# Moving the tail of a long depthwise convolution into a state space chunk loop, and taking the two halves of an output projection in the other order

## The chip, the cores and the metric

One core of one Trainium2 chip runs the whole program. The metric is the device time of one execution in microseconds (us), the median of several runs.

## What is computed

Two transformer blocks, for 256 tokens of width 1024. The change touches the mixer of the second block alone. Cut to that:

```python
def ssd_mixer(z, xbc, dt_raw, conv_w, conv_b, dt_bias, a_log, d_skip, norm_w):
    xbc = silu(causal_depthwise_conv(xbc, conv_w, conv_b))        # 4 taps
    xs, bm, cm = split(xbc, [1024, 1536])
    dt = softplus(dt_raw + dt_bias)
    y = ssd_chunked(xs, dt, -exp(a_log), bm, cm)                  # chunks of 128 tokens, 16 heads in 4 groups
    y = (y + d_skip * xs) * silu(z)
    yg = y.reshape(b, l, 4, 256)
    yg = yg * rsqrt(mean(yg * yg, -1) + EPS)                      # one norm per group of 256 columns
    return yg.reshape(b, l, 1024) * norm_w

def conformer_conv(u, conv_w, conv_b, ln_g, ln_b):
    a, g = split(u, 2)
    h = causal_depthwise_conv(a * sigmoid(g), conv_w, conv_b)     # 31 taps
    return silu(layer_norm(h) * ln_g + ln_b)                      # over all 1024 columns

def second_block(x, ...):
    proj = rmsnorm(concat([meta, x])) @ w_in                      # z, xbc, dt, conformer input
    h = h + concat([y_ssd, y_conf], -1) @ w_out                   # 2048 x 1024
    h = h + peer_ffn(rmsnorm(h), ...)
```

The rest (a first block with attention and a feed forward, then the expert layer with its 16384 experts) is as it was.

## The kernel before, in words

Activations lie transposed: 128 partitions of columns, 256 (or 272, with 16 meta tokens) tokens along a row, so 1024 columns are 8 tiles. All weights stream through in 423 **units** of 128x1024 numbers in one fixed order. SyncE loads a unit into one of four buffers (`load_weights`, L268), ScalarE rounds it to its high part (`hi_to`, L907), VectorE subtracts to get the low part (`lo_to`, L1360), and TensorE makes three products of high and low parts for each 128x128 block (`three`, L302 to L304), 24 matmuls of 256 tokens to a unit. Three slots `W` hold converted units: ScalarE may convert unit u when TensorE has ended unit u-3, and SyncE may load unit u when VectorE has ended unit u-4. Each engine has one program, written out by hand; nothing reorders it. An engine that waits holds up all that stands behind it.

The mixer's stages, in the order of the program (times of the next sections are from the profile's start):

- Units U_ZA, U_GLU, U_XB (40 units) make z, the conformer input `GP` and xbc. Beside them VectorE starts the long convolution: `long_convs` (L1609), one instruction of 128x256 per tap and tile, 156 in all. 18 of the 31 taps of tiles 4 and 5, and all of tiles 0 to 3, are VectorE's. TensorE does the other 88 taps (`PE_TAPS`: 13 of tiles 4 and 5, all 31 of tiles 6 and 7) as fp32 products with diagonal matrices (`conv_taps`, L615), which ScalarE makes (`diagonals`, L1145) from a ring of `NDIAG` = 64.
- The step sizes dt (L628, L1648 to L1655), their decays (L634 to L636), and then for the three pieces of tokens (16, 128, 128) the transposes of xs and B (L647, L656), scaled by VectorE (L1669, L1676), each followed by taps on TensorE (`tap(8)`) and on VectorE (`some_taps`).
- Chunk states (L673, copied at L1210, combined at L1684, L1687).
- The last taps; the layer norm of the conformer half: column sums for the mean (L682), subtraction (L1694), squares (L914), their sums (`column_sums`, L310), root (L920), inverse (L1366), scaling (L1698), silu and high part (L1222, L1224), low part (L1702).
- The **chunk loop**, n = 0 to 9: `core_a(n)` (L717 to L725) makes decay sums and C times B for one of 8 (group, chunk) pairs, ScalarE takes exponentials (L1235, L1237), VectorE multiplies (L1711, L1716), `core_b(n-1)` (L742, L744) makes the outputs, VectorE adds the skip and the gate (L1727, L1732). Between `core_a` and `core_b` stands one unit of the conformer half of the output projection (`conformer_units`). Every second turn a group is complete: squares, `group_sum` (L753), root, inverse, scaling (L1739), high and low part (L1251, L1742).
- Then the 8 units of the state space half of the output projection, which add into the same four accumulators ps0 to ps3, and the residual sum (L1749). The query projection (U_WQ) follows.

The lines that set the order around the change:

```python
            for n in range(10):
                if n < 8:
                    core_a(n)
                if n in (0, 1, 2, 4, 5, 6, 8, 9):
                    next(conformer)
                if 1 <= n < 9:
                    core_b(n - 1)
                if n >= 3 and n % 2:
                    group_sum((n - 3) // 2)
            for m in range(8):
                weights(U_OS + m)
```

## Time and profile before

| | |
|---|---|
| median of 3 runs | 1465.0 us (1464.36 to 1465.64) |
| the profiled execution | 1464.91 us, span 1462.8 us |
| TensorE busy | 1402.1 us, 96% of the span |
| VectorE busy | 1072.0 us, 73% |
| ScalarE busy | 736.5 us, 50% |
| the stretch that the change edits | 489 to 630 us of the span |

### The profile page before, as it was taken

Reading aid. Unit: us, or ns where it says so; the run is one execution under the profiler, and the core shown is the slowest. Engines: PE = TensorE matmul, PEld = TensorE weight load, DVE = VectorE, ACT = ScalarE, POOL = GpSimd, SP = SyncE. Lnnn points to the kernel's source line nnn. Section 1 sums busy time; section 2 is a strip of 40 time slices with the busy share of each in tenths; the row PEclk is TensorE's granted clock in tenths of the full one; section 3 lists DMA queues with packets and bytes.
Section 4 is the critical chain, followed back from the end, with each engine's and each line's share of the span. In section 5 each row is a group of like instructions: output and inputs, shape, how many; then the busy total and the mean of one; then the engine's idle time right before and its main releaser. Section 6 shows DMA issues by size and latency. Waiting matters only on the chain.

```text
span 1462.8 us, 25179 instructions
## 1 busy us (share of the span) xinstructions
PE 1402.1 (96%) x10456; PEld 1281.1 (88%) x10456; DVE 1072.0 (73%) x1742; ACT 736.5 (50%) x1051; POOL 3.1 (0%) x8
## 2 busy tenths in 40 slices
PE   6999899997999989899999999999999999999997
PEld 6978799997999867899999999999987777888886
DVE  7654766447799866677899986888878888655554
ACT  6755555445567535466544445443444344444443
POOL 0000000000000000000000000000000000000000
PEclk9999899998999899999999999999999999999999
DMA  7423355663555002355555555555455555656653
GB/s 259 157 73 106 116 183 177 210 191 103 183 162 168 18 0 73 101 174 160 175 185 188 173 188 182 166 167 165 159 172 163 171 163 169 180 191 201 188 186 105
DMA packets 63617, 228.59 MB, mean 156 GB/s; under 512 B 7312, under 2 KB 8208, under 8 KB 63376
## 3 DMA queue, kind: packets, MB, share of 16 engines
q1 hardware_dynamic: 63072, 226.25, 48.7%
q8 instruction: 82, 1.34, 0.4%
q10 hardware_dynamic: 432, 0.74, 0.1%
q14 instruction: 31, 0.25, 0.1%
HBM read 225.91 MB, written 1.05 MB: 155 GB/s over the span
## 4 chain that ended last, share of the span: by engine, by line
PE 89%; DVE 6%; ACT 4%; issue 1%; DMA 0%; DVEq 0%; ACTq 0%
PE ps L302 17%; PE ps L304 17%; PE ps L303 17%; PE ps L870 8%; PE ps L872 8%; PE ps L871 8%; PE ps L615 2%; PE ps L836 2%; DVE W L1360 1%; DVE RSI L1366 1%; PE ps L352 1%; ACT W L907 1%; PE ps L354 1%; PE ps L498 1%; PE ps L360 1%
## 5 line engine op out<-in xcount | busy, mean ns | idle before, releaser
L1360 DVE TENSOR_TENSOR W<-raw,W 128x1024 fp32r<-128x1024 f32 x423 | 515.6, 1222 | 275.1 <-ACT W L907 273.7
L907 ACT ACTIVATE W<-raw 128x1024 fp32r<-128x1024 f32 x423 | 446.3, 1057 | 393.7 <-PE ps L872 208.4
L302 PE MATMUL ps<-XH,W 128*128 128x256 f32 (+1 forms) x1552 | 442.4, 285 | 3.1 <-DVE hid L1780 2.0
L303 PE MATMUL ps<-XL,W 128*128 128x256 f32 (+1 forms) x1552 | 439.8, 283 | 0.0
L304 PE MATMUL ps<-XH,W 128*128 128x256 f32 (+1 forms) x1552 | 437.7, 282 | 0.0
L302 PEld LDWEIGHTS ps<-XH,W 128*128 128x128 f32 x1552 | 291.9, 188 | 5.0 <-DVE hid L1780 2.2
L304 PEld LDWEIGHTS ps<-XH,W 128*128 128x128 f32 x1552 | 294.0, 189 | 0.0
L303 PEld LDWEIGHTS ps<-XL,W 128*128 128x128 f32 x1552 | 292.6, 188 | 0.0
L870 PE MATMUL ps<-W,HH 128*128 128x512 f32 x512 | 205.7, 402 | 0.8 <-ACT hid L1325 0.8
L872 PE MATMUL ps<-W,HL 128*128 128x512 f32 x512 | 203.1, 397 | 0.0
L871 PE MATMUL ps<-W,HH 128*128 128x512 f32 x512 | 203.0, 397 | 0.0
L872 PEld LDWEIGHTS ps<-W,HL 128*128 128x128 f32 x512 | 96.5, 188 | 23.4
L870 PEld LDWEIGHTS ps<-W,HH 128*128 128x128 f32 x512 | 96.5, 188 | 23.0 <-issue 1.0
L871 PEld LDWEIGHTS ps<-W,HH 128*128 128x128 f32 x512 | 96.6, 189 | 22.0
L1325 ACT ACTIVATE hid<-ps 128x512 f32<-128x512 f32 x64 | 38.3, 598 | 115.1 <-PE ps L304 115.1
L302 PE MATMUL ps<-F1H,W 128*128 128x256 f32 x256 | 70.7, 276 | 0.0
L303 PE MATMUL ps<-F1L,W 128*128 128x256 f32 x256 | 70.7, 276 | 0.0
L304 PE MATMUL ps<-F1H,W 128*128 128x256 f32 x256 | 70.7, 276 | 0.0
L1609 DVE SCALAR_TENSOR_TENSOR plain<-plain,vec 128x256 f32<-128x256 f32 x156 | 64.9, 478 | 0.5 <-DVE small L1651 0.5
L1893 DVE TENSOR_TENSOR onehot<-RSI 128x1024 f16<-128x1024 f16 x64 | 44.2, 691 | 16.8 <-PE ps L836 15.7
L304 PEld LDWEIGHTS ps<-F1H,W 128*128 128x128 f32 x256 | 48.1, 188 | 0.0
L302 PEld LDWEIGHTS ps<-F1H,W 128*128 128x128 f32 x256 | 48.1, 188 | 0.0
(327 smaller groups left out, 1997.7 us busy)
## 6 DMA issues: line engine op xcount, KB each, us to landing
raw<-in_w_dn SPq DMA_DIRECT2D x128, 512.0 KB, 3.5
raw<-in_w_up SPq DMA_DIRECT2D x128, 512.0 KB, 3.5
raw<-in_w_ff SPq DMA_DIRECT2D x64, 512.0 KB, 4.3
raw<-in_w_in SPq DMA_DIRECT2D x57, 512.0 KB, 3.7
raw<-in_w_out SPq DMA_DIRECT2D x24, 512.0 KB, 3.4
raw<-in_w_q SPq DMA_DIRECT2D x16, 512.0 KB, 3.6
raw<-in_w_kv SPq DMA_DIRECT2D x4, 512.0 KB, 3.4
plain1a<-in_memT SPq DMA_DIRECT2D x1, 1024.0 KB, 10.8
```

Of the source, the lines that this page charges most:

```text
L302: e.matmul(out, wh, xh, start=first, stop=False, skip_group_check=shared)
L303: e.matmul(out, wh, xl, start=False, stop=False, skip_group_check=shared)
L304: return e.matmul(out, wl, xh, start=False, stop=last, skip_group_check=shared)
L615: e.matmul(ps[7 if j < 6 else 0][:, half(j)], DIAG[:, p % NDIAG, :], GP[:, j, 16 + k:272 + k], start=k == 0, stop=p + 1 == len(PE_TAPS) or ...
L870: e.matmul(ps[b][:, :], HH[:, c % 8, tok], wh, start=c == 0, stop=False)
L871: e.matmul(ps[b][:, :], HH[:, c % 8, tok], wl, start=False, stop=False)
L872: return e.matmul(ps[b][:, :], HL[:, c % 8, tok], wh, start=False, stop=c == 127)
L907: e.activation(W[:, u % NSLOT, 0, :], raw[:, u % NRAW, :], ACT.Copy).then_inc(s["hi"], 1)
L1325: e.activation(hid_[:, 256 * c - 256:256 * c + 256], ps[(c // 2) % 4][:, :], ACT.Gelu).then_inc(s["gl"], 1)
L1360: e.tensor_tensor(W[:, u % NSLOT, 1, :], raw[:, u % NRAW, :], W[:, u % NSLOT, 0, :], ALU.subtract).then_inc(s["lo"], 1)
L1609: e.scalar_tensor_tensor(CV[:, j, :], GP[:, j, 16 + k:272 + k], V("ccw", 31 * j + k), CV[:, j, :], ALU.mult, ALU.add).then_inc(cv[j], 1)
L1893: e.tensor_tensor(OA, pairs(IOTA, 128), at(0, 128), ALU.is_equal).then_inc(s["oa"], 1)
```

## The change

Nothing is computed otherwise; the same instructions stand in another order, in other buffers, but for two.

- The units' order: the state space half `U_OS` now precedes the conformer half `U_OC`.
- TensorE's taps: 18 (was 14) before the decays, none (was 12) after them, 5 (was 8) behind each of six transposes, and 6 in each turn of the chunk loop where a conformer unit stood, until the 88 are done in turn 6. Their banks are ps0 and ps1; `NDIAG` is 32 and ScalarE makes 1 diagonal per unit (was 2), then 10, 8, 6 and 6 per turn.
- VectorE's taps: 3 and 2 where 8 and 5 stood, none (was 12) before the states; then 2 + 2 in each turn of the loop, and the last 6 in turn 7.
- `LT` and `CM`, the loop's exponentials, get a place of their own (they lay in `CV`, the convolution's result), where `XH` and `XL` lie at other times.
- The loop has 9 turns and no projection unit. Group 0's and 1's roots are taken together in turn 5 (two table loads on ScalarE for both), group 2's in turn 8, group 3's behind the loop.
- Behind the loop come the state space units (`mixed_units`), one tile of activations after the other over all 8 output tiles. Between them stand the layer norm's mean (behind the first), group 3's sum (behind the second) and the squares' sums (behind the third), and on VectorE and ScalarE the rest of the layer norm and of groups 2 and 3 beside the units' conversions. The conformer units come last.

```diff
-U_ZA, U_GLU, U_XB, U_OC, U_OS, U_WQ, U_SK, U_DN, U_UP, NU = 93, 101, 117, 133, 141, 149, 165, 167, 295, 423
+U_ZA, U_GLU, U_XB, U_OS, U_OC, U_WQ, U_SK, U_DN, U_UP, NU = 93, 101, 117, 133, 141, 149, 165, 167, 295, 423
-NDIAG = 64
+NDIAG = 32
...
-            tap(14)
+            tap(18)
             e.wait_ge(s["dt_v"], 3)
...
-            tap(12)
...
-                    tap(8)
+                    tap(5)
...
+            def mixed_units():
+                for c in range(8):
+                    weights(U_OS + c)
+                    if c == 0:
+                        for j, n in ((4, 13), (5, 13), (6, 31), (7, 31)):
+                            e.wait_ge(cv[j], n)
+                        e.wait_ge(s["rs"], N_G + 2)
+                    if c % 2 == 0:
+                        e.wait_ge(s["yc_l"], c // 2 + 1)
                     for k in range(8):
+                        t = three(ps[k // 2][:, half(k)], slot(U_OS + c, slice(k * 128, k * 128 + 128)),
+                                  (YCH[:, c, :], YCL[:, c, :]), c == 0 and k % 2 == 0, False, True)
...
-            for n in range(10):
+            for n in range(9):
                 if n < 8:
                     core_a(n)
-                if n in (0, 1, 2, 4, 5, 6, 8, 9):
-                    next(conformer)
-                if 1 <= n < 9:
+                tap(6)
+                if n >= 1:
                     core_b(n - 1)
                 if n >= 3 and n % 2:
                     group_sum((n - 3) // 2)
+            tap(len(PE_TAPS))
+            mixed = mixed_units()
+            next(mixed)
+            layer_mean()
+            next(mixed)
+            group_sum(3)
+            next(mixed)
+            e.wait_ge(s["ltm"], 8)
+            column_sums(6, 256, HT, SQ_LN)
+            for _ in mixed:
+                pass
...
# VectorE, in the loop
+                some_taps(2)
+                if n >= 1:
...
+                some_taps(2)
+                if n == 5:
+                    group_norm(0)
+                if n == 6:
+                    group_low(0)
+                    group_norm(1)
+                if n == 7:
+                    group_low(1)
+                    for _ in convs:
+                        pass
```

**Order, place 1: VectorE in one turn of the chunk loop.** Before, turn 1 (L1711, L1716: products with the exponentials; L1360: low part of a conformer unit; L1727, L1732: skip and gate):

```order
L1711 TENSOR_TENSOR plain2<-plain2,ps6 128x512 [waits c_c,lt]
L1716 TENSOR_TENSOR plain2<-plain2 128x512 [waits cm]
L1360 TENSOR_TENSOR W<-raw,W 128x1024 [waits hi]
L1727 SCALAR_TENSOR_TENSOR plain2<-plain2,vec,ps7 128x128 [waits c_b]
L1727 SCALAR_TENSOR_TENSOR plain2<-plain2,vec,ps7 128x128
L1732 TENSOR_TENSOR plain2<-plain2 128x2x128 [waits cy]
```

Now, turn 1 (L1733, L1738, L1747 and L1752 are the same four; L1637 is a tap of the long convolution, of tiles 4 and 5):

```order
L1733 TENSOR_TENSOR LT<-LT,ps6 128x512 [waits c_c,lt]
L1738 TENSOR_TENSOR CM<-CM,plain2 128x512 [waits cm]
L1637 SCALAR_TENSOR_TENSOR plain2<-plain2,vec 128x256 [waits cv4]
L1637 SCALAR_TENSOR_TENSOR plain2<-plain2,vec 128x256 [waits cv5]
L1747 SCALAR_TENSOR_TENSOR plain2<-plain2,vec,ps7 128x128 [waits c_b]
L1747 SCALAR_TENSOR_TENSOR plain2<-plain2,vec,ps7 128x128
L1752 TENSOR_TENSOR plain2<-plain2 128x2x128 [waits cy]
L1637 SCALAR_TENSOR_TENSOR plain2<-plain2,vec 128x256 [waits cv4]
L1637 SCALAR_TENSOR_TENSOR plain2<-plain2,vec 128x256 [waits cv5]
```

The unit's conversion has gone, and two taps stand ahead of the wait for `c_b`, two behind the gate.

**Order, place 2: VectorE from the taps into the layer norm.** Before (L1694: the layer norm's subtraction; L1366, L1698: its inverse and scaling; L1702: low parts; L1711: first product of the chunk loop):

```order
L1609 SCALAR_TENSOR_TENSOR plain2<-plain2,vec 128x256 [waits cv5]
L1609 SCALAR_TENSOR_TENSOR plain2<-plain2,vec 128x256 [waits cv4]
L1609 SCALAR_TENSOR_TENSOR plain2<-plain2,vec 128x256 [waits cv5]
L1694 SCALAR_TENSOR_TENSOR plain2<-ps2,plain2 128x256 [waits ln_mm]
L1694 SCALAR_TENSOR_TENSOR plain2<-ps2,plain2 128x256 x7
L1366 RECIPROCAL RSI<-RSI 128x256 [waits rs]
L1698 SCALAR_TENSOR_TENSOR plain2<-plain2,vec,RSI 128x256 [waits ri]
L1698 SCALAR_TENSOR_TENSOR plain2<-plain2,vec,RSI 128x256 x7
L1702 TENSOR_TENSOR YCL<-plain2,YCH 128x512 [waits yc_h] x4
L1711 TENSOR_TENSOR plain2<-plain2,ps6 128x512 [waits c_c,lt]
```

Now, from the last turns on (L1747, L1752: last skip and gate; L1394, L1720: inverse and scaling of group 2; L1771: the layer norm's subtraction; L1725: group 2's low part):

```order
L1637 SCALAR_TENSOR_TENSOR plain2<-plain2,vec 128x256 [waits cv5]
L1637 SCALAR_TENSOR_TENSOR plain2<-plain2,vec 128x256 [waits cv4]
L1637 SCALAR_TENSOR_TENSOR plain2<-plain2,vec 128x256 [waits cv5]
L1747 SCALAR_TENSOR_TENSOR plain2<-plain2,vec,ps7 128x128 [waits c_b]
L1747 SCALAR_TENSOR_TENSOR plain2<-plain2,vec,ps7 128x128
L1752 TENSOR_TENSOR plain2<-plain2 128x2x128 [waits cy]
L1394 RECIPROCAL RSI<-RSI 128x256 [waits rs]
L1720 SCALAR_TENSOR_TENSOR plain2<-plain2,vec,RSI 128x256 [waits ri]
L1720 SCALAR_TENSOR_TENSOR plain2<-plain2,vec,RSI 128x256
L1771 SCALAR_TENSOR_TENSOR plain2<-ps5,plain2 128x256 [waits ln_mm]
L1771 SCALAR_TENSOR_TENSOR plain2<-ps5,plain2 128x256 x7
L1725 TENSOR_TENSOR YCL<-plain2,YCH 128x512 [waits yc_h]
```

The last taps moved behind the products of the last chunk, and between them and the layer norm's subtraction stand now the last skip and gate and the norm of group 2.

**Order, place 3: TensorE where the state space half begins and where a unit changes its accumulator.** Before, a unit of the projection in the loop, its end, `core_a` and the next unit's start (L302 to L304: the three products of a block; L717 to L725: `core_a`):

```order
L302 MATMUL ps0<-YCH,W 128x256
L303 MATMUL ps0<-YCL,W 128x256
L304 MATMUL ps0<-YCH,W 128x256
L717 MATMUL ps4<-plain2,cstb 128x512 [waits lt]
L718 MATMUL ps4<-MASK 128x512
L722 MATMUL ps5<-plain2,cst 128x512 [waits cm]
L725 MATMUL ps6<-plain2 128x128 [waits ltm]
L302 MATMUL ps0<-YCH,W 128x256 [waits lo]
L303 MATMUL ps0<-YCL,W 128x256
L304 MATMUL ps0<-YCH,W 128x256
```

Now, the end of the last `core_b` (L739, L741) and the first state space unit (L309 to L311 are the three products):

```order
L739 MATMUL ps7<-LT,plain2 64x128
L741 MATMUL ps7<-CM,plain2 64x128
L309 MATMUL ps0<-YCH,W 128x256 [waits cv7,cv6,rs,cv5,yc_l,cv4,lo]
L310 MATMUL ps0<-YCL,W 128x256
L311 MATMUL ps0<-YCH,W 128x256
L309 MATMUL ps0<-YCH,W 128x256
L310 MATMUL ps0<-YCL,W 128x256
L311 MATMUL ps0<-YCH,W 128x256
L309 MATMUL ps1<-YCH,W 128x256
L310 MATMUL ps1<-YCL,W 128x256
```

The first unit waits for the copies of the diagonal taps' sums, the third group's root and group 0's low part; the output half changes with every block and the accumulator with every second, where it was one accumulator for two whole units.

## Rows read from the trace of the kernel before

**Rows 1.** Section 1 of the page: busy us (share of the span) and instructions.

```profile
PE 1402.1 (96%) x10456; PEld 1281.1 (88%) x10456; DVE 1072.0 (73%) x1742; ACT 736.5 (50%) x1051; POOL 3.1 (0%) x8
```

**Rows 2.** Timeline of PE, decays to chunk loop (start, us, line, forms, [idle before <-releaser]).

```profile
489.85 7.12 PE L615 MATMUL ps<-plain,diag 128*128 128x256 f32 x24
496.81 0.60 PE L647 MATMUL ps<-cst,plain 128*16 128x128 f32 x4
497.24 3.62 PE L615 MATMUL ps<-plain,diag 128*128 128x256 f32 x16
500.70 0.60 PE L647 MATMUL ps<-cst,plain 128*16 128x128 f32 x4
...
521.14 3.91 PE L673 MATMUL ps<-plain 16*128 16x256 f32 x16
...
536.15 3.69 PE L310 MATMUL ps<-plain,cst 128*128 128x256 f32 x16 [1.60 <-ACT plain L914]
539.68 1.02 PE L717 MATMUL ps<-plain,cstb 128*128 128x512 f32 x2
```

**Rows 3.** Timeline of DVE: last taps behind the states, an inverse, a scaling.

```profile
526.95 2.06 DVE L1609 SCALAR_TENSOR_TENSOR plain<-plain,vec 128x256 f32<-128x256 f32 x5
...
569.03 1.75 DVE L1366 RECIPROCAL RSI<-RSI 128x256 f32<-128x256 f32 x1 [0.31 <-ACT RSI L920]
570.82 0.88 DVE L1739 SCALAR_TENSOR_TENSOR plain<-plain,vec,RSI 128x256 f32<-128x256 f32 x2
```

**Rows 4.** Timeline of PE, one turn of the chunk loop with its unit.

```profile
557.76 1.12 PE L717 MATMUL ps<-plain,cstb 128*128 128x512 f32 x2
...
559.94 0.36 PE L302 MATMUL ps<-YCH,W 128*128 128x256 f32 x1
...
562.86 0.45 PE L742 MATMUL ps<-plain 128*64 128x128 f32 x4
...
563.93 1.13 PE L717 MATMUL ps<-plain,cstb 128*128 128x512 f32 x2
```

**Rows 5.** Timeline of DVE, skip, gate and the next turn's products.

```profile
564.04 0.61 DVE L1727 SCALAR_TENSOR_TENSOR plain<-plain,vec,ps 128x128 f32<-128x128 f32 x2 [1.24 <-PE ps L744]
564.68 0.42 DVE L1732 TENSOR_TENSOR plain<-plain 128x256 f32<-128x256 f32 x1
...
566.46 0.69 DVE L1711 TENSOR_TENSOR plain<-plain,ps 128x512 f32<-128x512 f32 x1 [1.35 <-PE ps L725]
```

**Rows 6.** Timeline of ACT, a run of diagonals.

```profile
497.79 7.11 ACT L1145 ACTIVATE diag<-cst,vec 128x128 f32<-128x128 f32 x24
```

**Rows 7.** Waits of PE, 489 to 631 us (us in total, times, longest).

```profile
PE ps L302 <- DVE YCL L1702: 4.2, 1, 4.2
PE ps L302 <- DVE YCL L1742: 2.6, 1, 2.6
```

**Rows 8.** Windows (stretch; us, busy us by engine, granted clock, DMA share, GB/s).

```profile
535.00:540.00 5.00, 3.85 (x17) 3.34 (x18) 2.33 (x8) 2.64 (x5) 0.00 (x0) 1.00 0.01 3
...
545.00:550.00 5.00, 3.82 (x18) 3.85 (x18) 2.80 (x6) 4.82 (x12) 0.00 (x0) 0.50 0.00 0
...
608.20:613.20 5.00, 4.95 (x29) 4.95 (x30) 2.45 (x2) 1.28 (x2) 0.00 (x0) 0.66 0.38 116
...
127.80:139.40 11.60, 11.60 (x92) 10.38 (x90) 5.83 (x10) 5.63 (x12) 0.00 (x0) 1.00 0.43 136
```

**Rows 9.** Timeline of PE, two units, second to last matmul: mixed order, then one accumulator.

```profile
143.23 0.28 PE L303 MATMUL ps<-MXL,W 128*128 128x256 f32 x1
...
145.83 0.28 PE L304 MATMUL ps<-MXH,W 128*128 128x256 f32 x1
...
553.98 0.28 PE L303 MATMUL ps<-YCL,W 128*128 128x256 f32 x1
...
556.48 0.28 PE L304 MATMUL ps<-YCH,W 128*128 128x256 f32 x1
```

**Rows 10.** Timeline of DVE, the last residual sum.

```profile
629.93 0.69 DVE L1749 TENSOR_TENSOR X<-ps,X 128x512 f32<-128x512 f32 x1 [0.34 <-PE ps L304]
```

More of the change, by code:

```diff
@@ L159, in build @@
         P2b = stack()
-        DIAG = tensor(P2b, "diag", [128, NDIAG, 128])
+        diag_ = tensor(P2b, "diag", [128, 64, 128])
+        DIAG = [diag_[:, (16 if i < 16 else 32) + i, :] for i in range(NDIAG)]
         P2b.close()
@@ L166, in build @@
         DTU = [plain2[:, at:at + 2048].rearrange("p (a b) -> p a b", b=128) for at in (8 * 272, 16 * 272)]
-        LT, CM = (CV[:, 4 * i:4 * i + 4, :].rearrange("p (s a) b -> p s (a b)", s=2) for i in range(2))
         xb0 = 24 * 272 + 8 * 302 + 2048
@@ L1168, in scalar_program @@
                         conv_first(t)
-                for _ in range(2):
-                    next(diags)
+                next(diags)
             for m in range(16):
@@ L1179, in scalar_program, with diagonal @@
                                      scale=V("scw", 4 * i)).then_inc(s["xi"], 1)
-                for _ in range(2):
-                    next(diags)
+                next(diags)
+            def diagonal(n):
+                for _ in range(n):
+                    next(diags, None)
             for i in range(0, 16, 2):
@@ L1210, in scalar_program, with group_root, group_high @@
                 e.activation(PREV[0][:, hf * 512:hf * 512 + 512], ps[st_bank[hf]][:, :], ACT.Copy).then_inc(s["st_a"], 1)
-            conv_out(6, 31)
-            conv_out(7, 31)
-            sqrt_table()
+            def group_root(g):
+                root(N_G + g, g_bank[g], 256, 1.0 / 256, eps5, g % 2, 1 if g == 0 else 2)
+            def group_high(g):
+                for i in range(2):
+                    e.wait_ge(s["gn"], 2 * g + i + 1)
+                    e.activation(YCH[:, 2 * g + i, :], YC[:, 2 * g + i, :], ACT.Copy).then_inc(s["yc_h"], 1)
+            for n in range(9):
+                if n < 8:
+                    if n >= 2:
+                        e.wait_ge(s["c_b"], n - 1)
+                    e.wait_ge(s["c_d"], n + 1)
+                    e.activation(LT[:, n % 2, :], ps[4][:, :], ACT.Exp).then_inc(s["lt"], 1)
+                    e.wait_ge(s["c_a"], n + 1)
+                    e.activation(CM[:, n % 2, :], ps[5][:, :], ACT.Exp).then_inc(s["cm"], 1)
+                    diagonal(6)
+                if n == 2:
+                    hi_to(U_OS + 3)
+                if n == 5:
+                    group_root(0)
+                    group_root(1)
+                if n in (6, 7):
+                    group_high(n - 6)
+                if n == 7:
+                    conv_out(6, 31)
+                    conv_out(7, 31)
+                if n == 8:
+                    group_root(2)
+                if n >= 2 and n % 2 == 0:
+                    g = n // 2 - 1
+                    e.wait_ge(s["cy"], 6 * g + 6)
+                    square(SQ2[:, 2 * g:2 * g + 2, 0:256], YC[:, 2 * g:2 * g + 2, :])
+            group_high(2)
             for c in range(0, 8, 2):
                 e.wait_ge(s["ln_v"], c + 2)
-                square(SQ2[:, c:c + 2, 0:256], CV[:, c:c + 2, :])
-            root(N_LN, 3, 256, 1.0 / 1024, eps5)
+                square(HT[:, c:c + 2, 0:256], CV[:, c:c + 2, :])
+            hi_to(U_OS + 4)
+            group_root(3)
+            hi_to(U_OS + 5)
+            group_high(3)
+            hi_to(U_OS + 6)
+            root(N_LN, 6, 256, 1.0 / 1024, eps5, 0, 2)
             for j in range(8):
@@ L1733, in vector_program @@
                                     ALU.mult).then_inc(s["cy"], 1)
[L1734 to L1743 removed]
+                some_taps(2)
@@ new lines, in vector_program @@
+                if n == 2:
+                    lo_to(U_OS + 3)
+                if n == 5:
+                    group_norm(0)
+                if n == 6:
+                    group_low(0)
+                    group_norm(1)
+                if n == 7:
+                    group_low(1)
+                    for _ in convs:
+                        pass
+            group_norm(2)
+            e.wait_ge(s["ln_mm"], 1)
+            for j in range(8):
+                e.scalar_tensor_tensor(CV[:, j, :], ps[5][:, 0:256], -1.0 / 1024, CV[:, j, :], ALU.mult,
+                                       ALU.add).then_inc(s["ln_v"], 1)
@@ new lines, in vector_program @@
+            group_low(2)
+            lo_to(U_OS + 4)
+            group_norm(3)
+            lo_to(U_OS + 5)
+            group_low(3)
+            lo_to(U_OS + 6)
+            inverse(N_LN, 256)
+            for j in range(8):
+                e.scalar_tensor_tensor(CV[:, j, :], CV[:, j, :], V("lng", j), RI[:, 0, 0:256], ALU.mult,
+                                       ALU.mult).then_inc(s["ln_n"], 1)
+                if j in (3, 7):
+                    lo_to(U_OS + 7 + j // 4)
+            for j in range(0, 8, 2):
+                e.wait_ge(s["yc_h"], 8 + j + 2)
+                e.tensor_tensor(YCL[:, 8 + j:10 + j, :], CV[:, j:j + 2, :], YCH[:, 8 + j:10 + j, :],
+                                ALU.subtract).then_inc(s["yc_l"], 1)
```

174 lines of the change are left out of this document (60 added, 114 removed).

## The prediction

> **What bounds the kernel now.** I read the page first: TensorE is busy 96% of the span and VectorE 73% [rows 1], so a change of order can only win what TensorE loses between its matmuls. Next the windows and waits of the stretch that is edited: in 489 to 631 us TensorE waits 4.2 us once and 2.6 us once for low parts [rows 7], and behind each of these gaps its clock is granted at half for a while: 0.50 in 545 to 550 us, 0.66 in 608.2 to 613.2 us [rows 8]. Last the timelines of PE and DVE, which give every duration below. What the reader is to see in them: from 521.14 to 539.68 us TensorE does the last taps and the layer norm's sums, 18.5 us, for a chunk loop that needs none of it [rows 2]; and the loop then runs at TensorE's own pace, 6.17 us a turn [rows 4]. The layer norm's chain of short steps on three engines has nothing beside it but the start of the loop, and the last group's chain has nothing beside it at all.
>
> **The sum** is a new timetable for TensorE from 489.3 us (decays done) to its last matmul of the output projection, which is at 629.7 us now (0.2 to 0.3 us ahead of the residual sum that waits for it [rows 10]). Outside, nothing changes its length: ScalarE makes 32 diagonals fewer beside the units, where it isn't what is waited for; TensorE's four more taps ahead of the decays (1.7 us) end about when VectorE has the step sizes (the decays' products are through at 489.85 now, where the next taps start [rows 2]; I take 489.3 for both). Table loads on ScalarE fall by three, one comes back beside the query projection; both lie beside longer TensorE work, so I cost them at nothing. The DMA queue keeps its waits (unit u behind the low part of u-4); the new order gives it long stretches to fill four buffers, so nothing there either.
>
> *Prices.* A tap on TensorE: 8 in 500.70 - 497.24 = 3.46 us, 0.433 each. Four transposes: 497.24 - 496.81 = 0.43 us [rows 2]. A tap on VectorE: 2.06 / 5, 0.40 with pipelining. Inverse 1.75, scaling 0.88 [rows 3]. `core_a`: 559.94 - 557.76 = 2.18; a unit's 24 matmuls 2.72 (0.1135 each [rows 9]); `core_b`: 563.93 - 562.86 = 1.07 us [rows 4]. A product with an exponential 0.60, skip 0.6, gate 0.42 [rows 5]. A diagonal 7.11 / 24 = 0.30 [rows 6]. Handing over from TensorE to VectorE: 564.04, where the skip starts, against 563.93, where TensorE goes on behind the products it needs, so 0.1 and what one product of 64 rows takes: 0.25, an estimate.
>
> *A. Decays to chunk states.* Now 489.3 to 521.14 = 31.9 us, with 12 + 48 taps. The change leaves 30: 30 x 0.433 = 13.0 less, 18.9. VectorE's own chain here (two large products, then scalings with 3 or 2 taps between them) I walked through beside it: it holds the third transpose group back by some 0.3 net. 19.2 us: **-12.7**.
>
> *B. States to the first `core_a`.* Now 521.14 to 539.68 = 18.5 us. The new `core_a` waits for VectorE's fourth combination, which ended where its next taps start, 526.95 - 521.14 = 5.8 us behind the states' start [rows 2, 3]; with the hand-over 6.0: **-12.5**. TensorE idles 2.1 of them.
>
> *C. Chunk loop.* Now 539.68 to 608.25 us = 68.6 us, the second 2.6 us wait included, and 0.75 of a state space unit is done in it. New: turn 0 2.18 + 6 x 0.433 = 4.8; turns 1 to 5 each 2.18 + 2.60 + 1.07 = 5.85, 29.3; two group sums 1.7; turn 6 with 4 taps 5.0; turn 7 with a group sum 4.1; that is 44.9 us. Is it TensorE's pace? In a turn VectorE has 0.6 + 0.6, two taps 0.8, skip and gate 1.0, two taps 0.8: 3.8 of 5.85 us. It waits for `core_b` at the turn's end, and its four instructions behind that end 0.4 us before the next turn's `core_a` is through (2.18 us in), so turns 0 to 5 don't slip. ScalarE has two exponentials and 6 x 0.30: 2.8 us. From turn 5 on VectorE falls behind. From the end of turn 5's `core_b`: hand-over 0.3, skip and gate 1.0, taps 0.8, group 0's inverse and scaling 2.65; turn 6: 1.2 + 0.8 + 1.0 + 0.8, a low part 0.6, group 1's 2.65; turn 7: 1.2 + 0.8 + 0.6 for the skip that the last `core_b` must wait for: 14.4 us, where TensorE needs 10.0 (with its group sum) to be there. So it idles **4.6 us** ahead of the last `core_b` (1.07). 50.6 us; some 0.1 us a turn is lost where kinds of matmul change (6.17 now against 5.97 by the parts [rows 4]): 51.2. **-17.4** for this place.
>
> *D. Projection to its end.* Now 608.25 to 629.7 = 21.4 us. New: 16 units x 2.72 = 43.5; mean 3.5, squares' sums 3.5 (like L310's 3.7 [rows 2]), group sum 0.9: 51.4. Beside it VectorE ends the taps, the last gate, group 2's norm (1.0 + 2.65), the subtraction 2.75, and so on with the units' low parts between: walked through with ScalarE's squares and silu, it is late for the seventh unit by 0.3, for the eighth by 1.2 (ScalarE must first do five of the eight silus) and for the first conformer unit by 0.8: 2.3 us. The state space units run in mixed order. The first block's output projection does so too, and there 22 distances take 145.83 - 143.23 = 2.60 us, here 556.48 - 553.98 = 2.50 [rows 9]: 8 units x 24 x 0.0045 = 0.9. It may have another cause, so 0 to 0.9; I take 0.8, the same kind of unit. 54.5 us: **+33.1**.
>
> The clock: a gap of 1.60 us left it at 1.00 [rows 2, 8]; that of 2.6 was followed by 0.66 over 5 us (1.7 us of work lost), that of 4.2 by at least 0.50 over 5 us (2.5, and more behind it) [rows 7, 8]. For the new gap of 4.6 I take 2.6, with 1.7 to 5 as bounds; for the one of 2.1 ahead of the loop nothing, with 1.7 as upper bound. **+2.6**.
>
> Sum: -12.7 - 12.5 - 17.4 + 33.1 + 2.6 = -6.9 us. The profiled execution took 1464.9, the median is 1465.0: **1458.0**.
>
> The Trainium skill (TensorE: Matmul & The Clock Gate, "A second HAM failure mode: psum-queue depth-cycling") speaks against this change: a kernel that went through the PSUM banks in turn made TensorE idle a little between groups, often enough that its clock went up and down. In this case's trace the units in mixed order had 1.00 granted over 127.8 to 139.4 us [rows 8]; by the rule the eight mixed units would lose clock, and that is rival 4.
>
> **The rivals.**
>
> 1. *The forecast* (0.58): taps hidden in the loop, one exposed wait of VectorE at its end, clock down once. Its own range 1455.4 to 1460.4.
>
> 2. *More is won* (0.20): the clock stays up, or VectorE's lag at the loop's end is smaller, since I added its instructions up with their full durations. Without the clock's 2.6: 1455.4; with half the wait too: 1453.1. For it: the 1.6 us gap without a fall. Against: 4.6 is longer than both gaps that had one.
>
> 3. *VectorE is late all the way* (0.14). It is in order, and its conversions now stand behind norms; if each of the units 4 to 8 and the first conformer unit waits 0.5 us more and the clock falls twice, 3.0 + 1.7: 1462.7, hardly a gain. For it: by the same prices VectorE has about 27.7 us of work in the 29 us from the last tap to the first conformer unit.
>
> 4. *The clock in mixed order* (0.03). If bank changes made TensorE's clock alternate, half clock over half of 8 x 2.72 us costs 10.9: 1468.9; over all of it 21.8: 1479.8. Against: rows 8, the same pattern at 1.00.
>
> 5. *Slower: the loop turns at its round trip* (0.05). `core_a` frees its bank through ScalarE's exponential, the exponential stands behind six diagonals, VectorE's product behind four taps. If these lay on the circle, a turn would be 6.17 + 6 x 0.30 + 4 x 0.40 = 9.6 instead of 5.95, seven turns + 25.6: 1483.6. It decides from the point where ScalarE's or VectorE's work in a turn, with its one wait for TensorE, is longer than the turn of 5.9 us. ScalarE has 2.8 us, VectorE 3.8, and both start a turn's work while TensorE is in its taps, so I give it little.
>
> That the taps don't get into the loop at all is excluded: the order shows them there.
>
> **How the numbers follow.** 1458.0 is the likeliest case's. The range reaches from rival 2's middle to just short of rival 3's value, 1453.5 to 1462.5, and leaves out some 0.15. A measurement of this kernel can tell 0.2%, 2.9 us, from no change, so faster means under 1462.1: cases 1 and 2 whole and nearly two thirds of case 3, 0.87; same, the rest of 3: 0.05; slower, 4 and 5: 0.08.
>
> **What would show it.** Right: first `core_a` near 514.5 us; turns of 5.9 to 6.0 us, VectorE's products not late in turns 0 to 5; a wait of TensorE of 4 to 5 us for the skip's result ahead of the last `core_b`, near 560 us; half clock behind it for some 3 to 7 us; the last eight units back to back; the last residual sum near 623 us, 7 us earlier. Wrong: turns above 6.3 us; waits for low parts ahead of many units; half clock within the mixed units away from any gap; a difference outside this stretch of more than 1.5 us.

## The result, and the profile after

| | before | changed |
|---|---|---|
| median | 1465.0 us (7 runs on this chip) | 1459.68 us (7 runs, 1454.2 to 1463.2) |
| ratio | | 0.9953 (0.9934 to 0.9973) |
| profiled execution | 1464.91 us, span 1462.8 | 1459.68 us, span 1457.9 |
| forecast | | 1458.0 us (1453.5 to 1462.5) |

Faster by half a per cent, inside the range. The page of the changed kernel, busy times as in [rows 1]; and below it TensorE's windows of the four stretches of the forecast's sum (columns: stretch, its length, PE busy and matmuls, granted clock, DMA share, GB/s).

```profile
PE 1402.6 (96%) x10456; PEld 1281.4 (88%) x10456; DVE 1070.3 (73%) x1742; ACT 733.1 (50%) x1047; POOL 3.2 (0%) x8
```

```profile
494.05:513.12 19.07, 17.55 (x100) 1.00 0.00 1
513.12:519.12 6.00, 3.91 (x18) 1.00 0.00 0
519.12:570.29 51.17, 47.61 (x277) 0.99 0.03 11
570.29:625.45 55.16, 54.71 (x422) 0.97 0.43 134
sum 131.40, PE 123.78; mean PE 30.95
```

The stretch from the decays to the last residual sum takes 131.40 us. The same window of the kernel before:

```profile
489.25:629.93 140.68, 129.48 (x820) 0.95 0.17 57
```

So 9.3 us were won in it, where 6.9 were forecast. They are 3.6 us of idle time (11.2 before, 7.6 now) and 5.7 us of busy time; of the latter 1.7 are the four taps that moved ahead of the decays. The rest is clock: 0.95 over 140.68 us cost about 7 us (half clock in three places: behind the decays, and behind the waits of 4.2 and 2.6 us), and the one half-clock stretch left (0.53 in 569.9 to 573.3 us) costs 1.6; against it stand units that went 0.9 us slower (last section). PE's waits (us in total, times, longest) are all new. Those of before in this stretch (4.2 and 2.6 us for low parts, 1.6 and 1.3 for squares, 1.3 for roots, 0.2 for another) are gone:

```profile
PE ps L739 <- DVE plain L1747: 3.6, 1, 3.6
PE ps L716 <- issue: 2.1, 1, 2.1
PE ps L653 <- DVE plain L1697: 1.2, 1, 1.2
PE ps L309 <- DVE W L1388: 0.5, 1, 0.5
PE ps L662 <- DVE plain L1697: 0.3, 1, 0.3
```

The loop turns as the sum had it. PE's timeline of one turn, to be held beside [rows 4] (start, length, engine, line, operation, tiles, count):

```profile
529.85 1.13 PE L716 MATMUL ps<-plain,cstb 128*128 128x512 f32 x2
...
532.11 2.76 PE L622 MATMUL ps<-plain,diag 128*128 128x256 f32 x12
534.80 0.45 PE L739 MATMUL ps<-LT,plain 128*64 128x128 f32 x4
...
535.87 1.12 PE L716 MATMUL ps<-plain,cstb 128*128 128x512 f32 x2
```

A turn of 6.02 us, of which the six taps are 2.69 (532.11 to 534.80), and TensorE waits for nothing in it. At the loop's end VectorE's timeline shows what the last `core_b` (568.93) waits for: group 1's inverse and scaling stand between turn 6's gate and turn 7's products, with taps on both sides. VectorE has had no pause since turn 5's skip (554.90), so group 0's norm and the taps of turns 5 and 6 are in this lateness too.

```profile
562.22 0.87 DVE L1637 SCALAR_TENSOR_TENSOR plain<-plain,vec 128x256 f32<-128x256 f32 x2
563.01 0.68 DVE L1725 TENSOR_TENSOR YCL<-plain,YCH 128x512 fp32r<-128x512 f32 x1
563.62 1.74 DVE L1394 RECIPROCAL RSI<-RSI 128x256 f32<-128x256 f32 x1
565.39 0.88 DVE L1720 SCALAR_TENSOR_TENSOR plain<-plain,vec,RSI 128x256 f32<-128x256 f32 x2
566.19 0.68 DVE L1733 TENSOR_TENSOR LT<-LT,ps 128x512 f32<-128x512 f32 x1
```

Outside the stretch the profiled execution lost 4.8 us before it began (decays at 494.05 us instead of 489.25). PE's windows of the first block show it: the same two stretches of time, 10.2 us, first of the kernel before, then of the changed one.

```profile
54.20:61.00 6.80, 6.80 (x59) 6.80 (x60) 6.42 (x13) 5.94 (x10) 0.00 (x0) 1.00 0.46 151
81.60:85.00 3.40, 3.40 (x23) 2.25 (x24) 2.50 (x6) 0.84 (x3) 0.00 (x0) 1.00 0.33 107
```

```profile
54.20:61.00 6.80, 6.80 (x34) 6.80 (x34) 6.45 (x12) 5.63 (x10) 0.00 (x0) 0.50 0.49 151
81.60:85.00 3.40, 3.40 (x17) 3.40 (x17) 2.32 (x7) 1.15 (x4) 0.00 (x0) 0.50 0.02 7
```

(Columns here: PE, PEld, DVE, ACT and POOL busy, then the clock.) TensorE is busy throughout in both, at clock 1.00 before and 0.50 now: 10.2 us at half clock are 5.1 us of work lost. Ahead of the first place stand products of 6 columns (L421, from 52.83 us), ahead of the second a wait of 1.17 us; both stand in the kernel before as well, and its clock stayed at 1.00 there. The first question is whether that belongs to the change.

### The profile page after: what moved, and what is told of

It is laid out like the page before. It is cut to its first block, busy times and chain, and to the rows that moved or that the text cites. A ratio compares the mean times of both kernels' runs of the same rounds, so it can differ in the third digit from the quotient of the medians.

```text
span 1457.9 us, 25167 instructions
## 1 busy us (share of the span) xinstructions
PE 1402.6 (96%) x10456; PEld 1281.4 (88%) x10456; DVE 1070.3 (73%) x1742; ACT 733.1 (50%) x1047; POOL 3.2 (0%) x8
## 4 chain that ended last, share of the span: by engine, by line
PE 89%; DVE 7%; ACT 3%; issue 1%; DMA 0%; DVEq 0%; ACTq 0%
PE ps L309 17%; PE ps L310 17%; PE ps L311 17%; PE ps L880 8%; PE ps L882 8%; PE ps L881 8%; PE ps L846 2%; PE ps L622 2%; DVE W L1388 1%; DVE RSI L1394 1%; PE ps L359 1%; PE ps L361 1%; PE ps L505 1%; ACT W L917 1%; DVE plain L1637 1%
## 5 line engine op out<-in xcount | busy, mean ns | idle before, releaser
L309 PE MATMUL ps<-XH,W 128*128 128x256 f32 (+1 forms) x1552 | 443.6, 286 | 2.7 <-DVE hid L1825 2.0
L311 PE MATMUL ps<-XH,W 128*128 128x256 f32 (+1 forms) x1552 | 438.5, 283 | 0.0
L309 PEld LDWEIGHTS ps<-XH,W 128*128 128x128 f32 x1552 | 293.2, 189 | 4.7 <-DVE hid L1825 2.2
L311 PEld LDWEIGHTS ps<-XH,W 128*128 128x128 f32 x1552 | 295.1, 190 | 0.0
L309 PE MATMUL ps<-F1H,W 128*128 128x256 f32 x256 | 70.7, 276 | 0.0
L311 PE MATMUL ps<-F1H,W 128*128 128x256 f32 x256 | 70.7, 276 | 0.0
L1637 DVE SCALAR_TENSOR_TENSOR plain<-plain,vec 128x256 f32<-128x256 f32 x156 | 66.1, 478 | 0.0
L311 PEld LDWEIGHTS ps<-F1H,W 128*128 128x128 f32 x256 | 48.1, 188 | 0.0
L309 PEld LDWEIGHTS ps<-F1H,W 128*128 128x128 f32 x256 | 48.1, 188 | 0.0
## 6 DMA issues: line engine op xcount, KB each, us to landing
plain1a<-in_memT SPq DMA_DIRECT2D x1, 1024.0 KB, 10.6
```

The source lines that it names most:

```text
L309: e.matmul(out, wh, xh, start=first, stop=False, skip_group_check=shared)
L311: return e.matmul(out, wl, xh, start=False, stop=last, skip_group_check=shared)
L1637: e.scalar_tensor_tensor(CV[:, j, :], GP[:, j, 16 + k:272 + k], V("ccw", 31 * j + k), CV[:, j, :], ALU.mult, ALU.add).then_inc(cv[j], 1)
```

## The experiments

These kernels ran on other chips than the first comparison, the kernel before beside them each time; it had medians of 1467.6 to 1469.5 us there. So ratios are compared, and stretches of traces.

**The change again, and the kernel before again.** Nothing is edited.

> The changed kernel once more, with nothing edited. Theory (the edit's gain is the stretch from the decays to the last residual sum, 131.4 us against 140.7, and what was lost in the first block of the profiled execution, 4.7 us, is chance): the stretch again within 0.5 us of 131.4, from the last decay sum to the first core_a 25 us, the wait ahead of the last core_b 3.4 to 3.8 us; the time in the first block, which the edit doesn't touch, may come out otherwise. Rival (the new memory layout slows the first block each time): the first state space product again 4 to 5 us later than in the kernel before. Total 1454 to 1463 either way, median 1459.7.

> The kernel before once more, for its trace. Theory (half clock in the first block comes by chance and in either kernel, and is what makes one execution differ from the next): the stretch from the decays to the last residual sum within 0.7 us of 140.7 us, and where the total is above 1467, stretches of half clock ahead of 150 us that the first trace of this kernel didn't have, each of 3.4 us of them worth 1.7 us. Rival (only the changed kernel has them, through its other places in memory): none there, and a total of 1464 to 1467.

The change again: 1460.69 us, ratio 0.9941 (0.9918 to 0.9963); its stretch 132.21 us, 0.3 us outside what I expected, the wait ahead of the last `core_b` 3.6 us again. Its clock fell behind the 2.1 us gap ahead of the loop too (last section). The kernel before, one execution: 1469.78 us, its stretch 137.76, 2.2 us outside what I expected. Windows up to the decays and in the first block, of the kernel before in its first trace and then in this one (PE busy first, the clock third from the end):

```profile
0.00:489.25 489.25, 451.29 (x3533) 0.97 0.49 157
```

```profile
0.00:497.37 497.37, 461.35 (x3532) 0.95 0.50 155
...
53.50:60.30 6.80, 6.80 (x33) 6.80 (x34) 6.45 (x11) 5.93 (x10) 0.00 (x0) 0.50 0.38 122
80.80:84.20 3.40, 3.40 (x16) 3.07 (x17) 2.32 (x8) 1.15 (x4) 0.00 (x0) 0.51 0.18 72
```

The same two places at half clock, in the kernel before. And three kernels with the changed one's places in memory (both, best and order_only, below) have 1.00 in the two places. So the 4.8 us are not the change's: in 14 traces of these kernels the decays lie anywhere from 489.25 to 499.21 us. The stretch of the kernel before varies too, 140.68 and 137.76 us: half clock stood in three places of it in the first trace and in one, behind the 4.2 us wait, in the second. From pair to pair of traces the gain is therefore 5.6 to 9.3 us, and the 9.3 of the first pair are partly luck. The part that repeats is TensorE's idle time: 11.2 and 11.4 us before, 7.6 and 7.0 now.

**What the wait at the loop's end is.** Three kernels: group 1's norm later, VectorE's taps earlier, and both.

```diff
 # VectorE, norm_late (ScalarE's root of group 2 then precedes group 1's high part)
                 if n == 6:
                     group_low(0)
-                    group_norm(1)
                 if n == 7:
-                    group_low(1)
                     for _ in convs:
                         pass
+                    group_norm(1)
+            group_low(1)
             group_norm(2)
 # VectorE, taps_early: both calls in the chunk loop
-                some_taps(2)
+                some_taps(4)
```

> Group 1's inverse, scaling and low part are taken out from between turn 6 and turn 7's products and stand behind the last taps; ScalarE's part moves with them. Theory (TensorE's 3.6 us wait ahead of the last core_b is VectorE's lag, of which this norm is 2.6 us, and VectorE has no room behind it): the wait falls to about 0.9 us and the half clock behind it (1.7 us) goes, 5.3 us less up to there, but VectorE's backlog is as long as before, so that about 2.5 us of it come back as a wait for squares or low parts behind the layer norm's mean: 2 to 3.5 us less than the changed kernel, 1456 to 1458. Rival (the wait is only a matter of order, VectorE has room enough): all 5.3 us kept, 1454.4. Rival (no gain, the backlog takes it all back as another wait with its clock fall): 1459.7.

> VectorE's taps go 4 + 4 to a turn in place of 2 + 2, so that all 38 are done in turn 4 and none is left for turns 5 to 7; nothing else moves. Theory (VectorE idles about 2.1 us in each of turns 0 to 5, before the products and before the skip, and taps put there cost nothing, while turns 5 to 7 and the last six lose 1.6 + 1.6 + 0.8 us ahead of the last core_b and 3.2 behind it): turns stay within 0.15 us of 6.02, the wait of 3.6 us goes to 0 to 0.3, no half clock behind it, and no wait comes instead: 5 to 6 us less than the changed kernel, 1453.7 to 1454.7. Rival (round trip: four taps between product and skip, 1.6 us where 1.5 are idle, lie on the circle of the turn): turns longer by 0.8 us in turns 1 to 4, +3.2, so 1457 to 1458.

> The two edits together: four plus four taps to a turn, and group 1's norm behind turn 7's gate. Theory (with the taps gone, the 1.7 us that TensorE still waited ahead of the last core_b were this norm, which stands between turn 6's gate and turn 7's products, and VectorE now has 3.1 us of room ahead of the layer norm's mean): no wait above 0.3 us ahead of the last core_b, none for squares, and the stretch from the decays to the last residual sum 1.7 us shorter than with early taps alone (128.3 us), 126.6, or 125 where no half clock falls into it. In all 1.5 to 2 us under the early taps, near 1455. Rival (the layer norm's chain becomes the bound, so that the norm's 2.6 us come back as waits of the units for low parts, as in the run with the norm alone): the stretch 128 us or more, no gain.

| | median, us | ratio to before | stretch, us | PE idle in it, us |
|---|---|---|---|---|
| changed kernel again | 1460.69 | 0.9941 (0.9918 to 0.9963) | 132.21 | 7.0 |
| norm_late | 1455.16 | 0.9900 (0.9880 to 0.9921) | 129.08 | 7.2 |
| taps_early | 1456.73 | 0.9922 (0.9903 to 0.9940) | 128.31 | 5.3 |
| both | 1452.94 | 0.9897 (0.9873 to 0.9921) | 125.56 | 4.3 |

The waits of norm_late:

```profile
PE ps L309 <- DVE W L1389: 2.6, 3, 1.6
PE ps L716 <- issue: 2.1, 1, 2.1
PE ps L653 <- DVE plain L1698: 1.2, 1, 1.2
PE ps L739 <- DVE plain L1748: 1.0, 1, 1.0
```

As expected, the wait falls from 3.6 to 1.0 us, and 2.6 us (0.5 in the changed kernel) stand before units instead, because VectorE's backlog is what it was. What is won is the clock, which stays at 1.00 over the whole stretch, and 0.9 us from a quicker pace of the last eight units, which this kernel and all that follow except copies4 have beside the changed one (last section). The median came 0.8 us under the range that I expected. (The profiled execution, 1456.36 us, is 4.8 us under that of the change again: 3.1 in the stretch, and the rest behind it, where 683 to 688 us had 0.66 granted there and 1.00 here.) With taps_early the turns are still 6.02 us with eight of VectorE's taps in each, so the round trip is not the limit. But the wait was 1.7 us, not 0 to 0.3, and the median 2 us above the range: I had added VectorE's lag up from turn 5, while it is cleared at turn 6's skip, for which VectorE waits 0.63 us. After that skip come gate, low part, 2.6 us of norm and two products, and those alone are longer than what TensorE has to do until then:

```profile
566.91 0.61 DVE L1747 SCALAR_TENSOR_TENSOR plain<-plain,vec,ps 128x128 f32<-128x128 f32 x2 [0.63 <-PE ps L741]
...
568.50 1.74 DVE L1394 RECIPROCAL RSI<-RSI 128x256 f32<-128x256 f32 x1
570.28 0.88 DVE L1720 SCALAR_TENSOR_TENSOR plain<-plain,vec,RSI 128x256 f32<-128x256 f32 x2
571.08 0.68 DVE L1733 TENSOR_TENSOR LT<-LT,ps 128x512 f32<-128x512 f32 x1
```

The pair of edits bears this out: in `both` no wait is left at the loop's end, and its stretch is 125.56 us.

**The parts of the change undone.** VectorE's 38 taps of the loop back ahead of it; TensorE's 40 back ahead of it; and both back, which leaves of the change the new order of the projection and the norms, and three small things: the buffers, four more of TensorE's taps ahead of the decays, and eight more behind the states in place of the twelve directly behind the decays.

```diff
 # vec_back: VectorE
-                        some_taps(3)
+                        some_taps(8)
...
-                    some_taps(2)
+                    some_taps(5)
+            some_taps(17)
 # te_back: TensorE, and ScalarE's diagonals earlier
-                    tap(5)
+                    tap(8)
...
+            tap(len(PE_TAPS))            # behind the states
-            diagonal(10)
+            diagonal(18)
-                diagonal((8, 6)[c])
+                diagonal((16, 22)[c])
```

> One part undone: VectorE's 38 taps of the loop go back ahead of it, 8 and 5 between the scalings and 17 ahead of the combination of the states; all else as in the changed kernel. Theory (ahead of the loop TensorE waits for VectorE, in the loop it doesn't): the first core_a 9 to 11 us later behind the decays (25.1 us now), the wait ahead of the last core_b 1.5 to 2 us in place of 3.6, half clock once or twice behind the long gap: 7 to 12 us more in all, 1467 to 1472. Rival (VectorE's taps were beside other work in either place, and what was won is TensorE's alone): within 2 us of the changed kernel.

> The other part undone: TensorE does 8 taps behind each group of transposes and the last 22 behind the states, none in the loop, whose turns are then core_a and core_b alone; ScalarE makes the diagonals earlier. Theory (TensorE's taps cost their 0.433 us wherever they stand, but ahead of the loop only 2.1 us of them fit beside a wait; in the loop a turn without them, 3.35 us of TensorE's work, can't be used since VectorE has 3.8 us in it): from the decays to the first core_a 40 us in place of 25, turns of 4.0 to 4.3 us in place of 6.02, TensorE waiting in each; 5 to 8 us more in all, 1465 to 1468, more where its clock falls in the loop. Rival (round trip: the loop's pace is set by the circle TensorE, ScalarE, VectorE, TensorE, and the taps fill it): turns stay above 5 us, and 10 us or more are lost.

> Both parts undone together: TensorE's 38 taps and VectorE's 38 taps all stand ahead of the loop, as in the kernel before (8 and 8 or 5 to each group, the rest behind the states), so that of the change only the new order of the projection and the norms is left, and LT and CM's own place. Theory now (a tap costs TensorE 0.433 us wherever it stands; VectorE's taps are only in the way where TensorE's have been taken from beside them, so that moving the taps wins nothing, and all is won by the layer norm's chain and the last groups' norms standing beside units): first core_a 38 to 39 us behind the decays without a wait above 1.7 us in all; turns of 3.4 to 3.6 us; 3 to 3.5 us of waits in turns 6 to 8 from the two norms; the stretch 127 to 129 us, the total 1455 to 1458, no more than the changed kernel. Rival, the forecast's reasoning (the taps in the loop win by filling it): the stretch as long as in the kernel before less the layer norm's 5 to 6 us, 134 to 136 us, and 1463 or more in all.

| | median, us | ratio to before | stretch, us | PE idle in it, us |
|---|---|---|---|---|
| vec_back | 1468.18 | 1.0000 (0.9984 to 1.0016) | 138.77 | 14.7 |
| te_back | 1460.15 | 0.9931 (0.9905 to 0.9957) | 131.98 | 7.7 |
| order_only | 1453.30 | 0.9898 (0.9876 to 0.9920) | 127.13 | 4.6 |

vec_back came out about as expected: the first `core_a` comes 33.8 us behind the decays, 8.7 later, with 7.8 us of wait ahead of it and 4.5 ahead of transposes, and the whole gain is gone. te_back did not: I expected 5 to 8 us more, and there was nothing. PE's timeline of its loop, from one `core_b` to the next:

```profile
537.32 0.45 PE L741 MATMUL ps<-LT,plain 128*64 128x128 f32 x4
...
538.39 1.12 PE L718 MATMUL ps<-plain,cstb 128*128 128x512 f32 x2
...
540.87 0.45 PE L741 MATMUL ps<-LT,plain 128*64 128x128 f32 x4
...
544.62 0.45 PE L741 MATMUL ps<-LT,plain 128*64 128x128 f32 x4 [0.29 <-DVE plain L1749]
```

Turns of 3.55 and 3.75 us. I had put a turn with VectorE's 3.8 us of work at 4.0 to 4.3, but the engines hand over with nearly no loss. What the taps cost ahead of the loop, their absence gives back in it. Then order_only: 127.13 us for the stretch, as the theory had it, and a median of 1453.30, 1.7 us below its range and far from the rival's 1463. With all taps ahead of the loop, as in the kernel before, the kernel is as fast as the changed one or faster (its ratio is 0.9898; the changed kernel's were 0.9953, clearly apart, and 0.9941, where the ends of the intervals just meet), and its trace has less idle time. Its waits in the stretch:

```profile
PE ps L741 <- DVE plain L1750: 2.7, 1, 2.7
PE ps L653 <- DVE plain L1699: 1.1, 1, 1.1
PE ps L309 <- DVE W L1390: 0.5, 1, 0.5
PE ps L309 <- ACT RSI L933: 0.3, 1, 0.3
```

No 2.1 us ahead of the loop, since the last 22 taps stand there beside VectorE's work. The 1.1 us ahead of the third group of transposes (499.33 us) are still there. So moving the taps into the loop wins nothing measurable; the new order of the projection, with the layer norm and the last norms beside its units, wins all of it (the three small things above were not taken apart from it). VectorE's taps in the loop only mend what TensorE's in the loop broke: TensorE's taps ahead of the loop were the cover of VectorE's there. Alone in the loop, in te_back, VectorE's taps make its stretch 4.9 us longer than order_only's.

**Two versions on from there.** `best` is `both`, with five of TensorE's taps behind the states instead of ahead of them, and without VectorE's four taps behind its two large products. `order_norm` is order_only with group 1's norm later, and no tap moved.

> As the one before, and two things more: five of TensorE's taps go from ahead of the chunk states to behind them, and VectorE's four taps behind its two large products go into the loop. Theory (TensorE's idle 2.1 us ahead of the first core_a is VectorE's combination, beside which taps fit; its waits of 0.4 and 1.2 us for VectorE's scalings are four taps of 0.4 us ahead of them): the waits of 2.1, 1.2 and 0.4 us all go to under 0.3 us, and 3.2 to 3.7 us less than the run before in the stretch, 122 to 123 us; near 1451.5. Rival (the scalings are held up by the two large products of 4.5 us, not by the taps): the waits of 1.6 us in all stay, and only 2.1 us are won.

> The kernel with all taps ahead of the loop, and group 1's norm behind turn 7's gate. Theory (all that is left to win beside TensorE's own 121 us of the stretch are waits and half clock, and the 2.7 us wait ahead of the last core_b is that norm): the wait under 0.4 us, no half clock behind it, 1.1 us of wait left ahead of the transposes and 0.5 to 0.8 for low parts: the stretch 122.5 to 123.5 us in place of 127.1, in all 4 us less, 1449 to 1451, the same as the version with every tap edit. Rival (VectorE's backlog comes back behind the loop, as it did when only the norm was moved): a wait of 1 to 2.5 us for low parts of the units, the stretch 125 us, and no more than 2 us won.

best: 1450.67 us, ratio 0.9882 (0.9859 to 0.9906); order_norm: 1451.88 us, 0.9893 (0.9875 to 0.9911). Both beat both kernels, and are not told apart, nor clearly from order_only. PE's window of best:

```profile
494.54:615.96 121.42, 120.89 (x813) 101.84 (x813) 95.33 (x165) 69.12 (x144) 0.00 (x0) 1.00 0.22 66
```

One wait of 0.5 us is left, at full clock: this stretch is TensorE's own 121 us. order_norm has 123.44 us with 2.4 idle; its wait at the loop's end was 0.8 us where I expected under 0.4, and its median 0.9 us above the range.

**The round trip, with ScalarE loaded.** Copies that nobody reads are added; nothing is left out.

```diff
                     diagonal(6)
+                    for i in range(4):
...
+                        e.activation(spare[i % 2][:, 1024:2048], flat(XO)[:, 0:1024], ACT.Copy).then_inc(s["spare"], 1)
```

> Behind the diagonals of each of the eight turns ScalarE makes four copies of 128x1024 numbers that nobody reads, about 3.9 us in all; it idled 3.7 us of a turn of 6.0. Theory (a turn is as long as the longest engine's own work in it): ScalarE needs 0.5 + 0.5 + 1.85 + 3.9 = 6.7 us, and 0.55 more every second turn, so turns of 6.7 to 7.1 us in place of 6.02 and some 6 to 9 us more in all, 1466 to 1469. Rival (round trip: TensorE's work before the exponential adds to ScalarE's, 2.2 us of core_a and 1.1 of core_b): turns of 9 to 10 us, 24 to 30 us more, 1484 to 1490.

1469.62 us, ratio 1.0003 (0.9988 to 1.0017), the stretch 140.54 us, 9.1 more than the changed kernel's, part of it half clock behind the new waits. The first turns are still 6.02 us, not 6.7 to 7.1 as expected, while ScalarE falls behind by 0.5 us or more in each; then they lengthen, and TensorE waits 3.3 us for an exponential and 4.2 us at the end. That is an engine overfilled by its own work, not a sum around the circle.

**One more product ahead of the conformer units**, of 128 columns.

```diff
             for _ in mixed:
                 pass
+            e.matmul(ps[5][:, 0:128], ones, ident, start=True, stop=True)
```

> The changed kernel with one more product of 128 columns, that nobody reads, ahead of the first conformer unit. It asks what sets the distance of two matmuls in these eight units, 117.8 ns in three kernels and 113.3 in five with the same operands and places. Theory (it is how the two streams of weights and columns happen to stand when the units begin): the distance changes to about 113.3 ns, 0.85 us less over eight units, less the 0.2 us that the product takes. Rival (something that lasts, as places in memory or transfers beside it): 117.8 ns as before.

The total was 1456.94 us, in one execution. The last two residual sums, on VectorE, first of the changed kernel and then of this one:

```profile
619.80 0.69 DVE L1794 TENSOR_TENSOR X<-ps,X 128x512 f32<-128x512 f32 x1 [0.45 <-PE ps L311]
625.45 0.69 DVE L1794 TENSOR_TENSOR X<-ps,X 128x512 f32<-128x512 f32 x1 [0.45 <-PE ps L311]
```

```profile
616.82 0.69 DVE L1795 TENSOR_TENSOR X<-ps,X 128x512 f32<-128x512 f32 x1 [0.34 <-PE ps L311]
622.26 0.69 DVE L1795 TENSOR_TENSOR X<-ps,X 128x512 f32<-128x512 f32 x1 [0.34 <-PE ps L311]
```

Two units take 5.65 us there and 5.44 here, so a matmul 117.7 and 113.3 ns.

## Why the prediction was right, and where it wasn't

The time came out: 1458.0 forecast, 1459.68 measured. In part that is luck: in the profiled pair the stretch gained 2.4 us more than forecast, and ahead of it, where the forecast had nothing, 4.8 us were lost. By its own steps:

- **A.** 19.2 us forecast, 19.07 measured, and two errors cancel in it: 18.9 us of TensorE's work and 0.3 of waiting were forecast, 17.55 and 1.5 measured. The forecast priced each tap that leaves A at 0.433 us. But of A's 31.9 us before, some 3.5 ran at half clock, behind a wait of 1.53 us ahead of the decays, and the twelve taps that stood there took 6.96 us, 0.58 each (489.85 to 496.81 [rows 2]). I had looked for half clock behind the two long waits only. PE's window of the place, of the kernel before:

```profile
490.00:493.50 3.50, 3.50 (x10) 2.83 (x10) 3.50 (x2) 0.25 (x2) 0.00 (x0) 0.52 0.00 0
```

- **B, C.** 6.0 and 51.2 us forecast, 6.00 and 51.17 measured. In C errors cancel too. The wait ahead of the last `core_b` was 3.6 us, not 4.6: the forecast's own figures give 4.4 (14.4 less 10.0), VectorE's chain took 14.1 (554.79 to 568.93 us), and TensorE came to the place after 10.6, not 10.0. TensorE's own part of the loop was 47.6 us, 1 us more than forecast.
- **D.** 57.1 us with the clock's term, 54.9 measured (55.16 less what lies between the last matmul and the residual sum). VectorE's lateness for units (2.3 us forecast) was 0.5; half clock came once and cost 1.6 instead of 2.6; the conformer units took 0.8 us more, at 117.7 ns a matmul instead of 113.5.
- **The mixed order.** Its term of 0.8 us was about right in size and wrong in reason. Behind the first mixed unit, which ran at half clock, they went at 117.7 ns a matmul, but for the third, which went at 114.1; and the changed kernel's conformer units, in the old order, went at 117.7 too. Mixing doesn't cause it.
- **Rival 4**, from the Trainium skill (TensorE: Matmul & The Clock Gate, "A second HAM failure mode: psum-queue depth-cycling"), did not come: the only half clock in the 55 us behind the loop lies behind the 3.6 us gap (0.53 in 569.9 to 573.3 us), and norm_late, both, best and order_norm have 1.00 over the whole stretch with the same mixed units.
- **Rival 5**, the round trip: refuted by turns of 6.02 us in three fillings of VectorE (none, four and eight taps), and of 3.4 to 3.8 us without TensorE's taps.
- **Outside the stretch** I forecast less than 1.5 us and there were 4.8, half clock in the first block. It came in the second trace of the kernel before too. The first 7 runs of that kernel lay within 2.4 us and told nothing of it; its later ones reached from 1461.9 to 1472.9 us. The range had no term for this, and held the result because it was wide enough for other reasons.

**The step that failed** is, beside the half clock overlooked in A, the reading of the sum more than a term. A, B and C were booked as gains of 12.7, 12.5 and 17.4 us against a cost of 33.1, and rival 1 called it "taps hidden in the loop". But on an engine that is busy 96% of the time a tap is hidden nowhere; it costs 0.433 us in either place. What the change could win was TensorE's idle 11.2 us and its half clock, and I never split the 9 us that way, or asked which part of the change removes which wait. order_only shows it: the layer norm's 1.6 us, the low parts' 4.2 and 2.6, the squares' 1.3 and the roots' 1.3 all go with the projection's order alone, and the taps moved into the loop bring 2.1 us of new wait ahead of it. (Of the 1.5 us ahead of the transposes 1.1 is in order_only too, whose twelve taps directly behind the decays also stand elsewhere.) te_back says that TensorE's taps may stand in either place, and vec_back that VectorE's may not stay ahead of the loop once TensorE's have left it.

What stays open: how much of the medians' differences is half clock that comes by chance (the expected 4 us from order_only to order_norm were 3.7 in the stretch, but the ratios, taken on two chips, are 0.9898 and 0.9893), and what brings half clock on in one execution and not in the next, as in the first block.

## What to carry to other kernels

Where one engine is nearly always busy, write the account of a stretch as its own work, its waits and its lost clock, and give each part of a change the waits that it removes; gains booked by place cancel and hide who earned them. Before taking work from beside another engine's work, ask whose cover it was. And take several traces of the kernel before, since one may lack a loss of 5 us that the next has.

## What was not expected of the hardware

**The same units at two paces.** The eight conformer units (192 matmuls back to back, the same operands and places) went at 117.8 ns a matmul in the changed kernel, again and copies4, and at 113.3 ns in the nine other traces with the new order, and stayed at the one or the other to their end. The changed kernel has two traces, each other kernel one. With one small product ahead of the units it was 113.3, in a single trace, so that the product did it is not shown. It isn't the clock, which is 1.00 in both (602.5 to 625 us here, 600 to 622 us in one_more). What sets the pace as a run of units starts is open; it is worth 0.9 us per eight units.

**The same gap, with and without a fall of the clock.** TensorE idles 2.1 us ahead of the first `core_a` in seven traces: both of the changed kernel, norm_late, taps_early, both, copies4 and one_more. PE's windows right behind it, of the changed kernel run again and then of its first trace:

```profile
518.67:523.00 4.33, 4.33 (x10) 0.64 0.00 0
```

```profile
519.12:524.00 4.88, 4.88 (x20) 1.00 0.00 0
```

The clock fell behind it in taps_early as well (0.63), and not in the other four. Likewise the 2.6 to 2.7 us wait of the kernel before was followed by 0.66 once and by 1.00 once, and of its gaps of 1.5 to 1.6 us the one ahead of the decays had a fall behind it, the two ahead of the squares' sums had none. Every wait of 3.3 us or more in the stretch had a fall behind it or in it. So a gap of 1.5 to 3 us costs, beside itself, 1.7 us or nothing, and the same gap of the same kernel does either from one execution to the next: a part of the spread of the runs.
